# State outputs of an S5 layer: two channel groups in one f32 product of 128 partitions and 80 columns

## The chip, the core and the metric

The kernel runs on one core of a Trainium2 chip. The metric is the device time of one execution in microseconds (us). The engines of the core run side by side, each through its own list of instructions, and wait for one another only through semaphores: PE (TensorE, matrix products), DVE (VectorE), ACT (ScalarE), POOL (GpSimd) and SP (SyncE, which here only issues transfers). A product is two things on PE: a load of weights (the stationary operand, listed as PEld) and a stream of columns (the moving operand).

## The reference

One step of a hybrid encoder layer for 320 tokens (256 of a prompt, 64 of a running stream), model width 2048. After a norm, one projection gives q, k, v for eight heads of differential attention and the input u of an S5 state space model. Both results go through an output projection and a residual, and then through PEER, a mixture of 16,384 single-neuron experts. What the change touches is the S5 part:

```python
bu_r = jnp.einsum('blgp,gnp->blgn', uf, bbar_r)
bu_i = jnp.einsum('blgp,gnp->blgn', uf, bbar_i)
pr, pi, hr, hi = lax.associative_scan(combine, (a_r, a_i, bu_r, bu_i), axis=1)
...
y = (jnp.einsum('blgn,gpn->blgp', hr, c_re.astype(f32))
     - jnp.einsum('blgn,gpn->blgp', hi, c_im.astype(f32))
     + d_skip.astype(f32).reshape(SSM_GROUPS, SSM_P) * uf)
y = jax.nn.gelu(y.reshape(B, L, SSM_WIDTH))
```

There are 64 channel groups of 16 channels, and each drives a complex state of 64 numbers. The outputs also hold the final states.

## The kernel before

**The S5 part in chunks.** The 320 tokens are 40 chunks of 8 tokens. Within a chunk the outputs are a product of the chunk's own inputs with a matrix `Tm[:, g, :]` (8 tokens x 16 channels = 128 rows, 128 columns) for each group g. What comes from earlier chunks is a product of the state at the chunk's start with the output matrix times powers of the step. The state has 64 real and 64 imaginary numbers, and two groups share the 128 partitions: the even group has partitions 0 to 63, the odd one 64 to 127. `HCt` holds the states, first 32 group pairs of real parts, then 32 of imaginary parts, 40 chunks each. `CA[..][0]` and `CA[..][1]` are the real and imaginary output matrices of four group pairs at a time, in two buffers; DVE computes the first (`output_powers`), POOL the second.

So a group takes three f32 products into the same 40 columns of a PSUM bank: one over 128 rows (`Tm`) and two over its half of 64 rows (`CA` with `HCt`). That is `group_outputs` (L1600, L1601, L1602).

**The order.** The work of the front part is written out by hand along one index p. Step p is one quarter (512 columns) of a block of projection weights. Each weight is split into a high and a low part: ACT makes the high part of step p (`high_piece`, L497), DVE the low part (`front_low`, L864 on `w_parts`), and PE multiplies both with the tokens (`token_rows`, L1516 to L1522, eight products of 512 columns per step). `w_parts` has four buffers, so ACT can make the high part of step p once PE has done the token products of step p - 4. Everything else is hung on steps: each engine's loop over p asks which extra pieces belong to that step, and does them after its weight piece.

Around the change these are:
- steps 36 to 51: `own_kernels`, four f32 products of 32 columns with weights of 128x128 (L1546, L1547)
- steps 66 to 79: `kernels_moved` on PE (L1583) shifts one piece of `Tm` through PSUM, and `kernels_out` on ACT (L532) takes it out; piece i is moved in step 66 + i and taken out at ACT's turn 70 + i, and PE starts piece i only when piece i - 2 is out
- steps 74 to 76: `carry_inside` on DVE finishes the states of three of five segments (`HP`); step 77: `states_turned` (L1079) copies `HP` into `HCt`; steps 78, 79, 87, 91, ... 107: `output_powers`
- steps 80 to 111: two `group_outputs` a step on PE
- steps 81 to 89 and 101 to 109: the norms of the heads of q and of k, squares and roots on ACT, the rest on DVE
- steps 95, 96, 107, 108, 115: `y_out` on ACT, a gelu from PSUM into `Yb`; steps 109 and 116: `y_save`, eight transfers each, issued by ACT's queue. POOL fetches them back as `yT`.

Tiles live in one large array `experts` at fixed words, so a tile's place decides when it may be written.

Of the kernel before, what the change touches and what calls it, by code (L numbers as in the profile page):

```python
# [13 lines left out]
ACT = mybir.ActivationFunctionType  # L14
AX = mybir.AxisListType

P = 128
# [12 lines left out]
STEP = 8  # L30
# [55 lines left out]
def build(nc, io):  # L86
# [8 lines left out]
    with ctx:  # L95
# [152 lines left out]
        def bank(b, n=COLS):  # L248
            return psum[:, b, 0:n]
# [4 lines left out]
            u_out u_sv ug cbx in_out in_fold lam_e lam s5dt s5exp s5sin wx cbd k7mm k7o tm_mm tm tz  # L254
            wt_tr wt f_mm fs hp hc h_out ca cb y_mm y_gl y_sv0 y_sv1 y_in0 y_in1
            qsq hvar hstd q_ok k_ok qk_tr qkT v_out k_out cache zeros
# [75 lines left out]
        def _(sp):  # L332
# [91 lines left out]
        def _(pool):  # L424
# [16 lines left out]
            pool.wait_ge(S["k7o"], 3)  # L441
            pool.tensor_copy(Tm[:, :, P - SSM_P:], k7.rearrange("p (g n) -> p g n", g=GROUPS)).then_inc(S["tz"], 1)
# [4 lines left out]
            pool.wait_ge(S["hc"], 1)  # L447
            for x in range(8):
# [40 lines left out]
        def _(act):  # L489
# [18 lines left out]
            def project_out(c, n):  # L508

                (t0, r), m = TILES[n], NT * c + n  # L510
                if c < 4:
                    dst = (q_tok, k_tok)[c // 2][0:r, n, 512 * (c % 2):512 * (c % 2) + 512]
                else:
                    dst = v_tok[c - 4][0:r, n, :]
                act.wait_ge(S["w_used"], 4 * (8 + 4 * c + 4))
                if n < 2:
# [10 lines left out]
            def kernels_out(i):  # L527
                j, half = divmod(i, 2)
                n = SSM_P * (j + 1)
                act.wait_ge(S["tm_mm"], i + 1)  # L530
                act.wait_ge(S["tz"], 1)
                act.activation(Tm[0:n, 32 * half:32 * half + 32, 16 * j:16 * j + 16], psum[0:n, 6 + half, :].rearrange("p (g n) -> p g n", g=GP),  # L532
                               ACT.Copy).then_inc(S["tm"], 1)

            def squares(kind, n):

                r = TILES[n][1]
                m = NT * kind + n
                act.wait_ge(S["in_out"], NT * (2 * kind + 2))
                act.wait_ge(S["in_fold"], 2 * kind + 2)  # L540
                if m:
                    act.wait_ge(S["hvar"], m)
                else:
                    act.wait_ge(S["hc"], 1)
                act.activation(sq_head[0:r, :], (q_tok, k_tok)[kind][0:r, n, :], ACT.Square).then_inc(S["qsq"], 1)
# [6 lines left out]
            def y_out(f):  # L552

                trio, par = divmod(f, 2)
                k = min(12, GP - 12 * trio)
                act.wait_ge(S["y_mm"], min(3 * trio + 3, 8))
                if f == 0:
                    act.wait_ge(S["h_out"], 32)
                act.activation(Yb.rearrange("p (a b) c -> p b a c", b=2)[:, par, 12 * trio:12 * trio + k, :],
                               bank(4 + f % 4, CH * k).rearrange("p (g c) -> p g c", g=k),  # L560
                               ACT.Gelu_apprx_tanh).then_inc(S["y_gl"], 1)

            def y_save(half):
                act.wait_ge(S["y_gl"], 4 + 2 * half)
# [17 lines left out]
            def exponentials(u):  # L582
                n = u // HEADS
                act.wait_ge(S["s_mx"], u + 1)
                r, kk = TILES[n][1], KEYS_OF[n]
# [78 lines left out]
            for p in range(16, 4 * B_PQ + 1):  # L664
# [195 lines left out]
        def _(dve):  # L860
# [217 lines left out]
            def states_turned():  # L1078
                dve.tensor_copy(HCt.rearrange("p x (s c) -> p x s c", s=SEGS),  # L1079
                                HP[:, :, 0:SEG, :].rearrange("p s c x -> p x s c")).then_inc(S["hc"], 1)  # L1080

            def output_powers(x):

                rr, ri, cre, cim, ncim = ca_parts(x)
                dve.wait_ge(S["hc"], 1)
# [107 lines left out]
            for p in range(4 * B_PQ):  # L1193
# [294 lines left out]
        def _(pe):  # L1488
# [95 lines left out]

            def group_outputs(g):
                x, par, gp = g // 8, g % 2, g // 2
                fill = 2 * (gp // 12) + par
                if g == 0:
                    pe.wait_ge(S["tm"], 14)
                    pe.wait_ge(S["tz"], 2)  # L1590
                    pe.wait_ge(S["fs"], 6)
                    pe.wait_ge(S["hc"], 1)
                if g % 8 == 0:
                    pe.wait_ge(S["ca"], x + 1)
                    pe.wait_ge(S["cb"], 3 * x + 3)
                if gp % 12 == 0 and fill >= 4:
# [6 lines left out]
                if g % 8 == 7:  # L1603
                    ins.then_inc(S["y_mm"], 1)
# [119 lines left out]
            for p in range(4 * B_PQ):  # L1724
# [44 lines left out]
                if Y_AT <= p < Y_AT + 32:  # L1769
                    group_outputs(2 * (p - Y_AT))  # L1770
                    group_outputs(2 * (p - Y_AT) + 1)
                if QKT_AT <= p < QKT_AT + 6:
# [209 lines left out]
```

## Time and profile before

| | us |
|---|---|
| median of 3 runs | 2347.05 (2345.45 to 2352.65) |
| the profiled execution | 2347.72 |
| its span (first to last instruction) | 2345.9 |
| PE busy in the span | 2253.5 (96%) |
| DVE, ACT, POOL busy | 1678.6, 1091.8, 575.2 |

The profile comes from one execution. Its own time is 0.7 us above the median. Where a row has the form "start, length, engine, line, operation", the start is in us from the span's start. A product in f32 appears as two entries (x2). Products are pipelined: the length of one overlaps its successor, so that the cost of a product is read from one start to the next. A bracket at the end of a row tells how long the engine was idle before it and who ended the wait.

### The profile page before, as it was taken

The page shows a single profiled execution, that of the slowest core. Times are in us where ns is not written, and L with a number is a line of the kernel's source. Part 1 is how long each engine was busy: PE and PEld are TensorE (multiplying, and loading weights), DVE is VectorE, ACT ScalarE, POOL GpSimd, SP SyncE. Part 2 cuts the span into 40 slices and gives each one's busy share as a digit, 9 for nine tenths or more (in the row PEclk, how much of TensorE's full clock was granted, in tenths as well). Part 3 has the DMA queues.
Part 4 walks back from the last instruction along what each step waited for, and adds up shares of the span by engine and source line. Part 5 has one row for each costly group of instructions (what it writes and reads, how often), then busy time and mean ns, then how long its engine had stood idle before and what let it go on. Part 6 is the DMA issues. An engine that isn't in the chain of part 4 may idle for free.

```text
span 2345.9 us, 43355 instructions
## 1 busy us (share of the span) xinstructions
PE 2253.5 (96%) x17133; PEld 2158.4 (92%) x17133; DVE 1678.6 (72%) x2869; ACT 1091.8 (47%) x1999; POOL 575.2 (25%) x437
## 2 busy tenths in 40 slices
PE   7899999899899989999799999999999999999998
PEld 7785887779899989999799999999999999999998
DVE  7947864665455872886388888777678888777856
ACT  4234335654344544554344444444444444444444
POOL 3002320000176897559011111111001111111000
PEclk9999999999999999999899999999999999999999
DMA  6542235223343544776788988888778888888864
GB/s 226 120 113 73 90 94 197 96 90 126 144 161 127 171 156 159 242 219 219 237 320 329 360 335 306 311 307 335 270 274 335 342 326 323 313 323 318 311 213 153
DMA packets 128078, 537.69 MB, mean 229 GB/s; under 512 B 27648, under 2 KB 63920, under 8 KB 67216
## 3 DMA queue, kind: packets, MB, share of 16 engines
q1 hardware_dynamic: 61888, 358.62, 43.7%
q0 software_dynamic: 19200, 136.70, 14.0%
q10 hardware_dynamic: 46864, 40.71, 5.6%
q8 instruction: 77, 1.26, 0.2%
q14 instruction: 49, 0.40, 0.1%
HBM read 507.02 MB, written 28.38 MB: 228 GB/s over the span
## 4 chain that ended last, share of the span: by engine, by line
PE 61%; issue 19%; POOL 12%; DVE 5%; DMA 1%; ACT 1%; ACTq 0%; POOLq 0%; DVEq 0%
PE psum L1492 17%; PE psum L1494 17%; PE psum L1493 17%; POOL w_parts L473 12%; DVE experts L864 3%; PE psum L1516 2%; DVE w_parts L864 1%; PE psum L1518 1%; PE psum L1517 1%; DMA experts<-xs_tmp 1%; PE psum L1601 1%; PE psum L1600 1%; PE psum L1521 1%; PE psum L1602 1%; PE psum L1522 1%
## 5 line engine op out<-in xcount | busy, mean ns | idle before, releaser
L497 ACT ACTIVATE w_parts<-ring 128x512 fp32r<-128x512 f32 x1296 | 817.4, 632 | 1062.4 <-PE psum L1494 886.7
L864 DVE TENSOR_TENSOR w_parts<-ring,w_parts 128x512 fp32r<-128x512 f32 x1040 | 710.7, 695 | 477.5 <-ACT w_parts L497 467.3
L1492 PE MATMUL psum<-x_parts,w_parts 128*128 128x256 f32 (+1 forms) x2624 | 775.5, 296 | 30.2 <-POOL w_parts L473 13.6
L1494 PE MATMUL psum<-x_parts,w_parts 128*128 128x256 f32 (+1 forms) x2624 | 760.9, 290 | 0.0
L1493 PE MATMUL psum<-x_parts,w_parts 128*128 128x256 f32 (+1 forms) x2624 | 760.8, 290 | 0.0
L1492 PE MATMUL psum<-h_parts,w_parts 128*128 128x256 f32 x2048 | 582.0, 284 | 16.1 <-DVE h_parts L864 16.1
L1493 PE MATMUL psum<-h_parts,w_parts 128*128 128x256 f32 x2048 | 581.5, 284 | 0.0
L1494 PE MATMUL psum<-h_parts,w_parts 128*128 128x256 f32 x2048 | 581.4, 284 | 0.0
L1492 PEld LDWEIGHTS psum<-x_parts,w_parts 128*128 128x128 f32 x2624 | 504.5, 192 | 40.0 <-issue 17.4
L1493 PEld LDWEIGHTS psum<-x_parts,w_parts 128*128 128x128 f32 x2624 | 504.8, 192 | 0.7
L1494 PEld LDWEIGHTS psum<-x_parts,w_parts 128*128 128x128 f32 x2624 | 504.3, 192 | 0.0
L1492 PEld LDWEIGHTS psum<-h_parts,w_parts 128*128 128x128 f32 x2048 | 395.3, 193 | 16.7 <-issue 8.8
L473 POOL TENSOR_TENSOR w_parts<-ring,w_parts 128x512 fp32r<-128x512 f32 x256 | 358.5, 1414 | 208.7 <-ACT w_parts L497 203.2
L1493 PEld LDWEIGHTS psum<-h_parts,w_parts 128*128 128x128 f32 x2048 | 395.3, 193 | 0.0
L1494 PEld LDWEIGHTS psum<-h_parts,w_parts 128*128 128x128 f32 x2048 | 395.2, 193 | 0.0
L864 DVE TENSOR_TENSOR experts<-experts 128x256 f32<-128x256 f32 (+10 forms) x329 | 195.8, 605 | 8.2 <-ACT experts L626 2.9
L485 POOL DMA_INDIRECT experts<-in_peer_v,experts x64 | 73.8, 1153 | 480.1 <-DVE experts L1430 393.2
L485 POOL DMA_INDIRECT experts<-in_peer_u_rows,experts x64 | 73.3, 1145 | 460.6 <-DVE experts L1425 454.4
L1430 DVE SCALAR_TENSOR_TENSOR experts<-experts 128x2048 f32<-128x2048 f32 x63 | 147.7, 2345 | 0.0
L1425 DVE SCALAR_TENSOR_TENSOR experts<-experts 128x2048 f32<-128x2048 f32 x64 | 146.3, 2286 | 0.0
L864 DVE TENSOR_TENSOR experts<-psum,experts 128x1024 f32<-128x1024 f32 (+4 forms) x138 | 112.9, 854 | 13.6 <-PE psum L1494 12.4
L1516 PE MATMUL psum<-w_parts,x_parts 128*128 128x512 f32 x192 | 85.9, 447 | 9.6 <-DVE w_parts L864 9.1
(218 smaller groups left out, 1977.6 us busy)
## 6 DMA issues: line engine op xcount, KB each, us to landing
ring<-in_peer_u SPq DMA_DIRECT2D x128, 1024.0 KB, 4.8
ring<-in_peer_v SPq DMA_DIRECT2D x128, 1024.0 KB, 4.8
ring<-in_w_in SPq DMA_DIRECT2D x32, 1024.0 KB, 4.8
ring<-in_w_out SPq DMA_DIRECT2D x16, 1024.0 KB, 4.8
ring<-in_w_pq SPq DMA_DIRECT2D x16, 1024.0 KB, 4.9
g_tmp<-experts ACTq DMA_DIRECT2D x16, 1024.0 KB, 6.1
experts<-g_tmp ACTq DMA_DIRECT2D x16, 1024.0 KB, 6.7
experts<-in_xT SPq DMA_DIRECT2D x8, 640.0 KB, 9.0
```

The costliest lines, as they stand in the source:

```text
L473: pool.tensor_tensor(w_parts[:, q, 1, :], ring[:, k, 512 * q:512 * (q + 1)], w_parts[:, q, 0, :].bitcast(F32), ALU.subtract).then_inc(S["w ...
L485: pool.indirect_dma_start(rows[b], None, table, bass.IndirectOffsetOnAxis(ap=ids[:, k:k + 1], axis=0)).then_inc(S[f"gr{b}"], 16)
L497: act.activation(w_parts[:, q, 0, :], ring[:, b % SLOTS, 512 * q:512 * (q + 1)], ACT.Copy).then_inc(S["w_hi"], 1)
L864: return dve.tensor_tensor(out, a, b, op)
L1425: dve.scalar_tensor_tensor(row, row, 1.0, xs, ALU.mult, ALU.mult, accum_out=dots[:, k:k + 1]).then_inc(S["row_used"], 1)
L1430: dve.scalar_tensor_tensor(accs, row, coef[:, k:k + 1], accs, ALU.mult, ALU.add).then_inc(S["row_used"], 1)
L1492: pe.matmul(out, w_parts[:, q, 0, c], moving(0), start=start, stop=False)
L1493: pe.matmul(out, w_parts[:, q, 0, c], moving(1), start=False, stop=False)
L1494: return pe.matmul(out, w_parts[:, q, 1, c], moving(0), start=False, stop=stop)
L1516: pe.matmul(o, xh, w_parts[:, q, 0, :], start=dc == 0, stop=False)
L1517: pe.matmul(o, xh, w_parts[:, q, 1, :], start=False, stop=False)
L1518: pe.matmul(o, xl, w_parts[:, q, 0, :], start=False, stop=dc == DC - 1)
```

## The change

The states are laid out in two tiles `HB[0]` (real) and `HB[1]` (imaginary), with 80 columns for each group pair: the even group's 40 chunks in the first 40 columns on partitions 0 to 63, the odd group's in the last 40 on partitions 64 to 127, and zeros elsewhere. One product over 128 partitions then gives the sum for both groups, each in its own columns. `Tm` stays one product per group. Both copies are split by halves of the partitions: DVE copies the real parts, ACT the imaginary ones, and POOL writes the zeros. Since the tiles need room, `HP`, `Yb` and the order of the groups within `Tm` move, and some waits are added to guard the words that are used again.

```diff
-Q_NORM, Y_FILLS, O_NORM, O_TURN = (81, 101), (95, 96, 107, 108, 115, 115), (143, 157, 171), (167, 168, 169, 171, 174, 175)
+Q_NORM, Y_FILLS, O_NORM, O_TURN = (81, 101), (91, 95, 103, 107, 115, 115), (143, 157, 171), (167, 168, 169, 171, 174, 175)
...
-        HP = at(18432, SEGS * (SEG + 1), 2 * GP).rearrange("p (s c) x -> p s c x", s=SEGS)
+        HP = at(26320, SEGS * (SEG + 1), 2 * GP).rearrange("p (s c) x -> p s c x", s=SEGS)
-        HCt = at(0, 2 * GP, CH)
+        HB = [at(0, GP, 2 * CH), at(20480, GP, 2 * CH)]
-        Yb = at(20480, GROUPS, CH)
+        Yb = at(10752, GROUPS, CH)
...
+        def kernel_at(g):
+
+            return (g + GROUPS // 2) % GROUPS
+
+        def states_of(ri, par):
+
+            of = slice(64 * par, 64 * par + 64)
+            return (HB[ri][of, :, CH * par:CH * par + CH].rearrange("p x (s c) -> p x s c", s=SEGS),
+                    HP[of, :, 0:SEG, GP * ri:GP * ri + GP].rearrange("p s c x -> p x s c"))
...
             sp.dma_start(ckT, io["cache_k"]).then_inc(S["cache"], 16)
+            sp.wait_ge(S["y_sv0"], 16 * STEP)
+            sp.wait_ge(S["y_sv1"], 16 * STEP)
...
             pool.wait_ge(S["hp"], 1)
+            pool.wait_ge(S["tz"], 3)
+            for ri in range(2):
+                for par in range(2):
+                    if ri or par:
+                        pool.wait_ge(S["hz"], 2 * ri + par)
+                    pool.memset(HB[ri][64 * par:64 * par + 64, :, CH * (1 - par):CH * (1 - par) + CH], 0.0).then_inc(S["hz"], 1)
             pool.dma_start(io["states"][:, 0, :], HP[:, SEGS - 2, SEG, :]).then_inc(S["h_out"], 16)
...
+                if p == F_AT + 30:
+                    for par in range(2):
+                        act.wait_ge(S["hin"], 1)
+                        act.activation(*states_of(1, par), ACT.Copy).then_inc(S["hci"], 1)
                 if 0 <= p - TM_AT - 4 < 14:
                     kernels_out(p - TM_AT - 4)
...
             def states_turned():
-                dve.tensor_copy(HCt.rearrange("p x (s c) -> p x s c", s=SEGS),
-                                HP[:, :, 0:SEG, :].rearrange("p s c x -> p x s c")).then_inc(S["hc"], 1)
+                for par in range(2):
+                    dve.tensor_copy(*states_of(0, par)).then_inc(S["hc"], 1)
...
+                if p == F_AT + 28:
+                    dve.sem_inc(S["hin"], 1)
...
-                pr = slice(64 * par, 64 * par + 64)
-                out = psum[:, 4 + fill % 4, CH * (gp % 12):CH * (gp % 12) + CH]
-                pe.matmul(out, Tm[:, g, :], UG[:, g, :], start=True, stop=False)
-                pe.matmul(out, CA[x % 2][0][pr, gp % 4, :], HCt[pr, gp, :], start=False, stop=False)
-                ins = pe.matmul(out, CA[x % 2][1][pr, gp % 4, :], HCt[pr, GP + gp, :], start=False, stop=True)
+                out = psum[:, 4 + fill % 4, 2 * CH * (gp % 6):2 * CH * (gp % 6) + 2 * CH]
+                for par in range(2):
+                    pe.matmul(out[:, CH * par:CH * par + CH], Tm[:, kernel_at(2 * gp + par), :], UG[:, 2 * gp + par, :], start=par == 0, stop=False)
+                pe.matmul(out, CA[x % 2][0][:, gp % 4, :], HB[0][:, gp, :], start=False, stop=False)
+                ins = pe.matmul(out, CA[x % 2][1][:, gp % 4, :], HB[1][:, gp, :], start=False, stop=True)
```

(`F_AT` is 48 and `TM_AT` 66.) On PE, from the end of step 80's token products to the start of step 81's, before the change (L1600: `Tm`, L1601 and L1602: the states' real and imaginary products):

```order
L1522 MATMUL psum<-w_parts,x_parts 128x512
L1600 MATMUL psum<-experts 128x40 [waits hc,ca,fs,cb,tz,tm]
L1601 MATMUL psum<-experts 128x40
L1602 MATMUL psum<-experts 128x40
L1600 MATMUL psum<-experts 128x40
L1601 MATMUL psum<-experts 128x40
L1602 MATMUL psum<-experts 128x40
L1516 MATMUL psum<-w_parts,x_parts 128x512 [waits f_lo]
```

and with the change (L1631: `Tm`, L1632 and L1633: the states of both groups):

```order
L1551 MATMUL psum<-w_parts,x_parts 128x512
L1631 MATMUL psum<-experts 128x40 [waits hc,hci,hz,ca,fs,cb,tz,tm]
L1631 MATMUL psum<-experts 128x40
L1632 MATMUL psum<-experts 128x80
L1633 MATMUL psum<-experts 128x80
L1545 MATMUL psum<-w_parts,x_parts 128x512 [waits f_lo]
```

Six products became four, and the first also waits for the zeros (`hz`) and for ACT's copies (`hci`).

On ACT, turns 77 to 80, before (L497: high parts of the weights; L532: `Tm` pieces out of PSUM):

```order
L532 ACTIVATE experts<-psum 64x32x16 [waits tz,tm_mm]
L497 ACTIVATE w_parts<-ring 128x512 [waits w_used]
L532 ACTIVATE experts<-psum 80x32x16 [waits tz,tm_mm]
L497 ACTIVATE w_parts<-ring 128x512 [waits w_used]
L532 ACTIVATE experts<-psum 80x32x16 [waits tz,tm_mm]
L497 ACTIVATE w_parts<-ring 128x512 [waits w_used,slot0]
```

and with the change (L518 and L556 are the same two; L708 copies the imaginary states):

```order
L556 ACTIVATE experts<-psum 64x32x16 [waits tz,tm_mm]
L518 ACTIVATE w_parts<-ring 128x512 [waits w_used]
L708 ACTIVATE experts<-experts 64x32x40 [waits hin] x2
L556 ACTIVATE experts<-psum 80x32x16 [waits tz,tm_mm]
L518 ACTIVATE w_parts<-ring 128x512 [waits w_used]
L556 ACTIVATE experts<-psum 80x32x16 [waits tz,tm_mm]
```

The two copies stand between the high part of step 78 and piece 8 of `Tm`, and wait for DVE's `hin`.

## Rows read from the trace of the kernel before

**Rows 1.** The page: busy time by engine; the chain that ended last, by engine.

```profile
PE 2253.5 (96%) x17133; PEld 2158.4 (92%) x17133; DVE 1678.6 (72%) x2869; ACT 1091.8 (47%) x1999; POOL 575.2 (25%) x437
...
PE 61%; issue 19%; POOL 12%; DVE 5%; DMA 1%; ACT 1%; ACTq 0%; POOLq 0%; DVEq 0%
```

**Rows 2.** Busy time by stretch: PE, PEld, DVE, ACT, POOL, clock, DMA share, GB/s.

```profile
243.29:358.66 115.37, 115.37 (x633) 98.60 (x632) 80.12 (x116) 37.05 (x57) 27.19 (x19) 1.00 0.26 85
...
320.00:335.00 15.00, 15.00 (x84) 12.78 (x83) 14.43 (x24) 6.00 (x9) 3.63 (x3) 1.00 0.00 1
```

**Rows 3.** Order of time, PE, step 81: start us, us, engine, line, operation.

```profile
245.00 0.50 PE L1516 MATMUL psum<-w_parts,x_parts 128*128 128x512 f32 x1
...
246.95 0.31 PE L1600 MATMUL psum<-experts 128*128 128x40 f32 x2
...
247.75 0.42 PE L1600 MATMUL psum<-experts 128*128 128x40 f32 x2
...
248.10 0.41 PE L1601 MATMUL psum<-experts 64*128 64x40 f32 x2
...
248.66 0.50 PE L1516 MATMUL psum<-w_parts,x_parts 128*128 128x512 f32 x1
```

**Rows 4.** Order of time, PE, a step with four full-height f32 products.

```profile
118.25 0.30 PE L1546 MATMUL psum<-experts 128*128 128x32 f32 x2
...
119.06 0.48 PE L1516 MATMUL psum<-w_parts,x_parts 128*128 128x512 f32 x1
...
120.96 0.30 PE L1546 MATMUL psum<-experts 128*128 128x32 f32 x2
```

**Rows 5.** Order of time, PE, f32 products of other shapes.

```profile
40.81 4.47 PE L1529 MATMUL psum<-experts 128*128 128x320 f32 x16
...
160.38 0.67 PE L1571 MATMUL psum<-experts 128*64 128x40 f32 x16
```

**Rows 6.** Order of time, steps 76 to 79, and one stretch.

```profile
223.47 2.54 DVE L864 TENSOR_TENSOR experts<-experts 128x448 f32<-128x448 f32 x5
...
225.57 1.02 PE L1583 MATMUL psum<-experts,ident 128*96 128x512 f32 x2
...
230.31 1.05 ACT L545 ACTIVATE experts<-experts 128x1024 f32<-128x1024 f32 x1
...
236.00 0.79 PE L1516 MATMUL psum<-w_parts,x_parts 128*128 128x512 f32 x1 [3.23 <-DVE w_parts L864]
...
239.57 1.91 PE L1583 MATMUL psum<-experts,ident 128*112 128x512 f32 x2
...
236.00:241.00 5.00, 5.00 (x11) 3.36 (x11) 4.93 (x5) 1.19 (x2) 2.50 (x2) 0.50 0.60 210
```

**Rows 7.** Order of time, steps 88 to 110, and one stretch.

```profile
263.19 1.28 DVE L864 TENSOR_TENSOR w_parts<-ring,w_parts 128x512 fp32r<-128x512 f32 x2
...
301.14 0.73 DVE L864 TENSOR_TENSOR w_parts<-ring,w_parts 128x512 fp32r<-128x512 f32 x1 [4.98 <-ACT w_parts L497]
...
301.14:343.45 42.31, 42.31 (x234) 36.11 (x232) 37.01 (x54) 14.78 (x21) 11.69 (x9) 1.00 0.29 86
...
311.00 0.50 PE L1516 MATMUL psum<-w_parts,x_parts 128*128 128x512 f32 x1
...
338.18 5.56 ACTq L566 DMA_DIRECT2D y_tmp<-experts  x8
...
344.45 1.29 DVE L864 TENSOR_TENSOR w_parts<-ring,w_parts 128x512 fp32r<-128x512 f32 x2 [1.00 <-ACT w_parts L497]
```

**Rows 8.** Order of time: POOL's fill and first powers, the saved outputs, SP.

```profile
185.93 6.94 POOL L439 MEMSET experts<- 128x8192 f32 x1 [158.96 <-PE psum L1555]
...
229.21 1.49 POOL L452 TENSOR_TENSOR experts<-experts 128x512 f32<-128x512 f32 x1 [11.37 <-DVE experts L1079]
...
370.22 0.76 POOL L463 DMA_DIRECT2D experts<-y_tmp  x1 [22.99 <-DMA y_tmp<-experts]
...
390.94 0.42 SPq L366 DMA_DIRECT2D experts<-in_cache_k  x1
```

More of the change, by code:

```diff
@@ L254, in build @@
             u_out u_sv ug cbx in_out in_fold lam_e lam s5dt s5exp s5sin wx cbd k7mm k7o tm_mm tm tz
-            wt_tr wt f_mm fs hp hc h_out ca cb y_mm y_gl y_sv0 y_sv1 y_in0 y_in1
+            wt_tr wt f_mm fs hp hin hc hci hz h_out ca cb y_mm y_gl y_sv0 y_sv1 y_in0 y_in1
             qsq hvar hstd q_ok k_ok qk_tr qkT v_out k_out cache zeros
@@ L441, in _ @@
             pool.wait_ge(S["k7o"], 3)
-            pool.tensor_copy(Tm[:, :, P - SSM_P:], k7.rearrange("p (g n) -> p g n", g=GROUPS)).then_inc(S["tz"], 1)
+            for half in range(2):
+                pool.tensor_copy(Tm[:, kernel_at(32 * half):kernel_at(32 * half) + 32, P - SSM_P:],
+                                 k7[:, 512 * half:512 * half + 512].rearrange("p (g n) -> p g n", g=GP)).then_inc(S["tz"], 1)
             pool.wait_ge(S["hp"], 1)
+            pool.wait_ge(S["tz"], 3)
[4 more added lines that the diff above has]
+                    pool.memset(HB[ri][64 * par:64 * par + 64, :, CH * (1 - par):CH * (1 - par) + CH], 0.0).then_inc(S["hz"], 1)
             pool.dma_start(io["states"][:, 0, :], HP[:, SEGS - 2, SEG, :]).then_inc(S["h_out"], 16)
             pool.dma_start(io["states"][:, 1, :], HP[:, SEGS - 1, SEG, :]).then_inc(S["h_out"], 16)
-            pool.wait_ge(S["hc"], 1)
+            pool.wait_ge(S["hz"], 4)
+            pool.wait_ge(S["hc"], 2)
             for x in range(8):
@@ L515, in project_out @@
                 act.wait_ge(S["w_used"], 4 * (8 + 4 * c + 4))
+                if c == 2 and n == 0:
+                    act.wait_ge(S["hc"], 2)
+                    act.wait_ge(S["h_out"], 32)
                 if n < 2:
@@ L531, in kernels_out @@
                 act.wait_ge(S["tz"], 1)
-                act.activation(Tm[0:n, 32 * half:32 * half + 32, 16 * j:16 * j + 16], psum[0:n, 6 + half, :].rearrange("p (g n) -> p g n", g=GP),
+                act.activation(Tm[0:n, kernel_at(32 * half):kernel_at(32 * half) + 32, 16 * j:16 * j + 16], psum[0:n, 6 + half, :].rearrange("p (g n) -> p g n", g=GP),
                                ACT.Copy).then_inc(S["tm"], 1)
@@ L543, in squares @@
                 else:
-                    act.wait_ge(S["hc"], 1)
+                    act.wait_ge(S["hc"], 2)
                 act.activation(sq_head[0:r, :], (q_tok, k_tok)[kind][0:r, n, :], ACT.Square).then_inc(S["qsq"], 1)
@@ L552, in y_out @@
             def y_out(f):
[L554 to L560, printed above, removed]
+                k = min(6, GP - 6 * f)
+                act.wait_ge(S["y_mm"], -(-(6 * f + k) // 4))
+                act.activation(Yb[:, 12 * f:12 * f + 2 * k, :], bank(4 + f % 4, 2 * CH * k).rearrange("p (g c) -> p g c", g=2 * k),
                                ACT.Gelu_apprx_tanh).then_inc(S["y_gl"], 1)
             def y_save(half):
-                act.wait_ge(S["y_gl"], 4 + 2 * half)
+                act.wait_ge(S["y_gl"], 3 + 3 * half)
                 for j in range(STEP):
@@ L584, in exponentials @@
                 act.wait_ge(S["s_mx"], u + 1)
+                if u == 0:
+                    act.wait_ge(S["y_sv0"], 16 * STEP)
+                    act.wait_ge(S["y_sv1"], 16 * STEP)
                 r, kk = TILES[n][1], KEYS_OF[n]
@@ L1078, in states_turned @@
             def states_turned():
-                dve.tensor_copy(HCt.rearrange("p x (s c) -> p x s c", s=SEGS),
-                                HP[:, :, 0:SEG, :].rearrange("p s c x -> p x s c")).then_inc(S["hc"], 1)
+                for par in range(2):
+                    dve.tensor_copy(*states_of(0, par)).then_inc(S["hc"], 1)
             def output_powers(x):
                 rr, ri, cre, cim, ncim = ca_parts(x)
-                dve.wait_ge(S["hc"], 1)
+                dve.wait_ge(S["hc"], 2)
                 if x >= 2:
@@ L1583, in kernels_moved, with pair_outputs @@
                 pe.matmul(psum[0:n, 6 + half, :], ident[:, P - n:P], k7[:, 512 * half:512 * half + 512], start=True, stop=True).then_inc(S["tm_mm"], 1)
[L1585 to L1588, printed above, removed]
+            def pair_outputs(gp):
+                x, fill = gp // 4, gp // 6
+                if gp == 0:
                     pe.wait_ge(S["tm"], 14)
-                    pe.wait_ge(S["tz"], 2)
+                    pe.wait_ge(S["tz"], 3)
                     pe.wait_ge(S["fs"], 6)
-                    pe.wait_ge(S["hc"], 1)
-                if g % 8 == 0:
+                    pe.wait_ge(S["hz"], 4)
+                    pe.wait_ge(S["hc"], 2)
+                    pe.wait_ge(S["hci"], 2)
+                if gp % 4 == 0:
                     pe.wait_ge(S["ca"], x + 1)
                     pe.wait_ge(S["cb"], 3 * x + 3)
-                if gp % 12 == 0 and fill >= 4:
+                if gp % 6 == 0 and fill >= 4:
                     pe.wait_ge(S["y_gl"], fill - 3)
-                pr = slice(64 * par, 64 * par + 64)
-                out = psum[:, 4 + fill % 4, CH * (gp % 12):CH * (gp % 12) + CH]
-                pe.matmul(out, Tm[:, g, :], UG[:, g, :], start=True, stop=False)
-                pe.matmul(out, CA[x % 2][0][pr, gp % 4, :], HCt[pr, gp, :], start=False, stop=False)
-                ins = pe.matmul(out, CA[x % 2][1][pr, gp % 4, :], HCt[pr, GP + gp, :], start=False, stop=True)
-                if g % 8 == 7:
+                out = psum[:, 4 + fill % 4, 2 * CH * (gp % 6):2 * CH * (gp % 6) + 2 * CH]
[3 more added lines that the diff above has]
+                ins = pe.matmul(out, CA[x % 2][1][:, gp % 4, :], HB[1][:, gp, :], start=False, stop=True)
+                if gp % 4 == 3:
                     ins.then_inc(S["y_mm"], 1)
@@ L1769, in _ @@
                 if Y_AT <= p < Y_AT + 32:
-                    group_outputs(2 * (p - Y_AT))
-                    group_outputs(2 * (p - Y_AT) + 1)
+                    pair_outputs(p - Y_AT)
                 if QKT_AT <= p < QKT_AT + 6:
```

## The prediction

> **What bounds the kernel now.** I read the page's totals first: PE is busy for 96% of the span, and the chain of waits that ended last lies 61% on PE [rows 1]. So time taken off PE shortens the run wherever PE waits for nobody. Next the table by stretch: from 243.29 to 358.66 us, which are the 32 steps 80 to 111 with the state outputs, PE is busy for all of 115.37 us at the clock's upper level (1.00, 2.4 GHz), and DVE for 80.12 [rows 2]. PE bounds that stage alone. DVE's part isn't even, though: from 320 to 335 it is busy for 14.43 of 15 us [rows 2]. What PE gives back elsewhere can be lost to DVE there.
>
> Then one step in the order of time. Step 81 begins at 245.00 with its token products, begins its group products at 246.95 and ends at 248.66: 1.95 + 1.71 = 3.66 us [rows 3]. The 1.71 us hold six products (three for each group), each shown as two entries. One costs 0.24 to 0.35 us: the second full-height product starts at 247.75, and its successor of 64 rows at 248.10 [rows 3].
>
> **The change part by part. The products.** Six products a step become four: two of 40 columns as before, and two of 128 rows and 80 columns. No row of before has that form. The nearest is the stage at 118 us, where a step holds four f32 products with weights of 128x128 and 32 columns: they take 118.25 to 119.06 = 0.81 us, and the whole step 2.71 [rows 4]. Do 80 columns cost more than 32? Sixteen entries of 320 columns are busy for 4.47 us [rows 5], 0.28 us each or 0.87 ns a column, so that 80 columns stream for 0.07 us; an entry of the 0.81 us takes 0.10. The weights and not the columns set the pace, and 0.81 stands. The ends: below, sixteen entries with weights of 64 columns are busy for 0.67 us [rows 5], so eight take 0.34; above, four times the slowest full-height spacing, 4 x 0.35 = 1.40 us [rows 3]. I take 0.81, since its rows have the weights' shape and the count. A step then takes 1.95 + 0.81 = 2.76 us instead of 3.66, and 32 steps lose 32 x 0.90 = **28.8 us** (32 x 0.31 = 9.9 and 32 x 1.37 = 44 at the ends).
>
> That 64-row products beside each other could be worth more than full-height ones is what the Trainium skill says against this change: by "TensorE: Matmul & The Clock Gate", section "Part 3: Packing small matmuls — row/col tiling", a weight load slides under a running product only where the two use different row groups, and products in different row groups run together. The trace shows no such pairs before, since a full-height product stands between the two halves; the rows at 118 us have full-height loads one after the other at 0.10 us. If the rule held for the new form, the products would take the upper end above.
>
> **The wait at step 76.** ACT now copies the imaginary states in two pieces, at its turn 78, and waits there until DVE has finished the last segment. DVE's five operations from 223.47 take 2.54 us, so this ends at 226.01 [rows 6]. A copy of 1024 columns takes 1.05 us [rows 6], two of 1280 about 2.6, so ACT comes to the Tm piece at 228.7 and has it out at 229.3. PE's Tm product of step 76 started at 225.57 [rows 6] and needs this piece's bank: PE stands still for 3.7 us. Queued behind it on ACT are the Tm pieces and the high parts of the next steps. But PE already stood still 3.23 us before step 79 until 236.00, for DVE, and DVE is not later [rows 6]. The new idle eats the old one: after it the clock is at the lower level, 0.50 (1.2 GHz), as it was from 236 to 241 after the old idle [rows 6]; steps 77 and 78 run slowly instead of step 79, and PE comes to step 79 at about 237.6, done with it at 240.5 instead of 239.57. The last Tm piece is late by that, and the first pair starts at some 244.2 instead of 243.29: **+0.9 us**. Ends: 0, if DVE's 236.00 decides as before, and 3.7 + 2.5 = 6.2, if the idle and a fall of the clock come on top (a fall: the token part of step 79 took 236.00 to 239.57 = 3.57 instead of 1.95, the Tm product 1.91 instead of 1.02 [rows 6]).
>
> **DVE and ACT behind shorter steps.** Steps 81 to 89 (head norms of q): DVE had the low parts of steps 88 and 89 by 263.19 + 1.28 = 264.47, one after the other, so 88's by 263.85 [rows 7]. PE would come to step 88 at 244.2 + 0.81 + 7 x 2.76 = 264.3: just in time, nothing lost. Steps 99 to 109 (k): DVE began step 99's low part at 301.14, 9.86 us before PE began that step at 311.00 [rows 7]. From there to 343.45 it was busy 37.0 us [rows 7]; with about 1 us of gaps between instructions that is 38.0, its work for 11 steps, while PE will need 11 x 2.76 = 30.4. Its head start spans four buffers and shrinks by 4 x 0.90 to 6.3. So it comes to step 110's low part 38.0 - 6.3 = 31.7 after PE's step 99 and has it at 32.4; PE would want it at 30.4. ACT's eight DMA issues (5.56 us from 338.18) stand before its high part of step 110, which made DVE wait 1.00 us more, until 344.45 [rows 7]. Together **+3.0 us**, in two to four short stalls from step 104 to 110. The ends: 0, and 6 if POOL's products, which run beside DVE's, hit it harder than before.
>
> **At nothing.** DVE's turning copy keeps its element count (half the partitions, two pieces). POOL's four fills, some 1.1 us each by 6.94 us for 8192 columns, begin when the carried state is ready; there POOL was idle for 11.37 us up to 229.21 [rows 8], which hides their 4.4. Without that cover the first powers would be late by as much. The two Tm copies on POOL are the old one in halves. Two more table loads on ACT (the gelus moved to steps 91, 95, 103 and 107) cost it 2.6 us where DVE is later than ACT. On SP, the wait for the saved outputs stands before cache_v, the v outputs and the first w_out block: the save landed before 370.22, SP came there at 390.94 [rows 8], so 20 us cover it. The transfers from y back to yT follow PE's step 111 as before.
>
> **Sum.** -28.8 + 0.9 + 3.0 = -24.9 us, from the profiled execution's 2347.7 (span 2345.9) to 2322.8. The median of the runs is 2347.05, 0.7 less, so I say 2322. The following stages start from PE's step 112 and shift as a whole.
>
> **Rivals.** (1) DVE becomes the bound and the clock falls: stalls at 104 to 110 as long as the 3.23 us after which the clock was at 0.50 [rows 6] cost 2.5 each; two of them and 3 us more of DVE save 17 and give 2330. For it: DVE's 14.43 of 15 [rows 2]; against: the stalls come out near 1 us. (2) The full-height loads don't overlap: 9.9 - 0.9, no stall, 2338. Against it the rows at 118 us. (3) No stall at all: 2318; POOL and DVE would have to collide less. (4) The change doesn't do what it says, as where 80 columns cost what three products did: 2347, for which no row speaks. (5) Slower: short steps starve PE so often that the clock stays at 0.50 within the stage. A step then takes 3.57 + 2 x 0.81 = 5.2 us, 1.5 above today's; from 12 of the 32 steps on the gain is gone, and with 20 it is -0.9 x 12 + 1.5 x 20 = +19, 2366. Against it: a PE at half speed lets DVE catch up, so that the idle ends by itself.
>
> **Numbers.** Forecast 0.64 (its own range 2316 to 2328), rival 1 0.15, rival 2 0.08, rival 3 0.05, rival 4 0.04, rival 5 0.04. From 2315 to 2332 lie the forecast, rival 3 and most of rival 1: 0.82. A difference under 0.3% (7 us) can't be told from none: faster 0.92, the same 0.04, slower 0.04.
>
> **What would show it.** A step of the stage at 2.7 to 2.8 us with eight f32 entries in about 0.81; the idle of 3 to 4 us before the Tm product of step 76 and none left before step 79; the first pair near 244; PE waits for DVE of about a microsecond between steps 104 and 110; step 112 at about 334 instead of 358.66. An entry of 80 columns well above 0.10 us makes the forecast wrong, as does a stage in which DVE ends most of PE's waits.

## The result and the profile after

The changed kernel takes 2336.17 us (median of 6 runs, 2328.09 to 2337.88), the kernel before in the same rounds 2347.14 us. The ratio is 0.9942 (95%: 0.9929 to 0.9954), which is 13.6 us; the two medians are 11.0 us apart. The forecast was 2322, a gain of 24.9 us, with a range up to 2332. So about half of the gain came, and the time lies outside the range.

The profiled execution has 2328.09 us, the fastest of the six, so it shows less of what is missing than the median has; the run named again below gives a second profile. The page, busy time and the chain (compare [rows 1]):

```profile
PE 2223.3 (96%) x17005; PEld 2133.7 (92%) x17005; DVE 1676.9 (72%) x2870; ACT 1098.3 (47%) x2003; POOL 583.7 (25%) x442
...
PE 58%; issue 19%; POOL 12%; DVE 7%; DMA 1%; ACT 1%; ACTq 1%; POOLq 0%; DVEq 0%
```

PE lost 30.2 us of busy time, but the span only 19.7 (2345.9 to 2326.2); DVE's share of the chain rose from 5% to 7%. First the part that came out as forecast, one step of the stage in order of time (start, length, engine, line; L1631 Tm, L1632 and L1633 the two new products; compare [rows 3]):

```profile
247.52 0.53 PE L1631 MATMUL psum<-experts 128*128 128x40 f32 x4
247.89 0.43 PE L1632 MATMUL psum<-experts 128*128 128x80 f32 x2
248.15 0.39 PE L1633 MATMUL psum<-experts 128*128 128x80 f32 x2
248.33 0.47 PE L1545 MATMUL psum<-w_parts,x_parts 128*128 128x512 f32 x1
...
250.25 0.53 PE L1631 MATMUL psum<-experts 128*128 128x40 f32 x4
```

The f32 products take 247.52 to 248.33 = 0.81 us, a step 2.73. So the loss isn't in the products. Busy time by stretch (columns as in [rows 2]; the first row is the stage and compares with the first of [rows 2], the last row with its second):

```profile
244.67:339.34 94.67, 88.57 (x505) 76.83 (x506) 77.95 (x116) 38.35 (x58) 29.50 (x19) 0.98 0.31 100
...
255.00:265.00 10.00, 9.97 (x60) 8.62 (x59) 9.64 (x15) 1.42 (x4) 4.64 (x3) 1.00 0.26 80
265.00:275.00 10.00, 7.28 (x36) 6.16 (x37) 9.72 (x15) 4.11 (x7) 6.06 (x3) 0.90 0.09 31
...
270.00:275.00 5.00, 2.74 (x14) 2.26 (x13) 4.79 (x11) 0.63 (x1) 1.25 (x1) 0.81 0.05 8
...
275.00:285.00 10.00, 10.00 (x55) 8.56 (x54) 7.43 (x9) 2.46 (x4) 4.24 (x3) 0.92 0.53 194
285.00:320.00 35.00, 35.00 (x207) 30.66 (x206) 27.97 (x35) 19.87 (x28) 12.91 (x10) 1.00 0.19 64
320.00:335.00 15.00, 11.65 (x66) 9.83 (x65) 12.94 (x28) 3.05 (x6) 0.07 (x1) 1.00 0.51 115
```

PE has two holes. From 265 to 275 it is busy for 7.28 of 10 us and the clock's mean falls to 0.90, where DVE is full (9.72); from 320 to 335 it is busy for 11.65 of 15. In between DVE has slack. The beginnings of these holes, PE in order of time:

```profile
265.46 0.50 PE L1545 MATMUL psum<-w_parts,x_parts 128*128 128x512 f32 x1 [0.49 <-DVE w_parts L891]
...
273.42 0.79 PE L1545 MATMUL psum<-w_parts,x_parts 128*128 128x512 f32 x1 [2.26 <-DVE w_parts L891]
...
322.65 0.50 PE L1545 MATMUL psum<-w_parts,x_parts 128*128 128x512 f32 x1 [1.03 <-DVE w_parts L891]
...
326.62 0.50 PE L1545 MATMUL psum<-w_parts,x_parts 128*128 128x512 f32 x1 [1.01 <-DVE w_parts L891]
...
333.64 0.50 PE L1545 MATMUL psum<-w_parts,x_parts 128*128 128x512 f32 x1 [1.31 <-DVE w_parts L891]
```

These are steps 88, 90, 107, 108 and 110. The last three are the short stalls forecast for steps 104 to 110. The first two were not forecast. What DVE and POOL do ahead of them (DVE's rows, then POOL's):

```profile
253.98 6.08 DVE L891 TENSOR_TENSOR experts<-experts,small 128x1024 f32<-128x1024 f32 x6
...
261.35 2.01 DVE L891 TENSOR_TENSOR experts<-experts 128x512 f32<-128x512 f32 x3
...
266.20 5.80 DVE L891 TENSOR_TENSOR experts<-experts,small 64x1024 f32<-64x1024 f32 x6
...
272.67 1.29 DVE L891 TENSOR_TENSOR w_parts<-ring,w_parts 128x512 fp32r<-128x512 f32 x2
...
254.16 2.03 POOL L473 TENSOR_TENSOR experts<-experts 128x512 f32<-128x512 f32 x1 [16.31 <-PE psum L1633]
...
265.12 1.87 POOL L473 TENSOR_TENSOR experts<-experts 128x512 f32<-128x512 f32 x1 [5.39 <-PE psum L1633]
```

The same pieces in the kernel before, which the prediction had not read together:

```profile
252.43 3.42 DVE L864 TENSOR_TENSOR experts<-experts,small 128x1024 f32<-128x1024 f32 x6
...
257.83 4.00 DVE L864 TENSOR_TENSOR experts<-experts 128x512 f32<-128x512 f32 x3
...
327.10 6.30 DVE L864 TENSOR_TENSOR experts<-experts,small 128x1024 f32<-128x1024 f32 x6
...
256.21 1.14 POOL L452 TENSOR_TENSOR experts<-experts 128x512 f32<-128x512 f32 x1 [17.63 <-PE psum L1602]
...
329.55 1.11 POOL L452 TENSOR_TENSOR experts<-experts 128x512 f32<-128x512 f32 x1 [9.83 <-PE psum L1602]
```

Before, the second q norm was over at 252.43 + 3.42 = 255.85 and POOL began its set at 256.21. POOL is released by PE, and the faster PE released it at 254.16; DVE, which began the stage later, came to the norm at 253.98. Now they run side by side and the norm takes 6.08 us. The third q norm meets the next set too (5.80). After it come the low parts of steps 90 and 91 (from 272.67), for which PE has waited 2.26 us.

The meeting itself isn't new, and its price stood in the trace before: there POOL's set at 256.21 ran beside DVE's own `output_powers` (4.00 us; 2.01 in the changed kernel), and its last set, from 329.55, beside the second k norm (6.30 us). PE filled the stage, so neither cost time. In the changed kernel the k norms take 3.41, 4.23 and 3.39 us, and DVE's busy time in the stage is even lower (77.95 us against 80.12). What changed is where the stretch falls. The second q norm's 2.66 us more are made up at once by the shorter powers and low part behind it: from its start to the low parts of steps 88 and 89 DVE needs 10.75 us (253.98 to 264.73), as before (252.43 to 263.19). The third norm's 2.4 us aren't made up before step 90's low part.

The beginning of the stage, ACT and PE (compare [rows 6]):

```profile
225.07 4.83 ACT L708 ACTIVATE experts<-experts 64x1280 f32<-64x1280 f32 x2 [6.10 <-DVEq L1286]
229.92 0.59 ACT L556 ACTIVATE experts<-psum 80x512 f32<-80x512 f32 x1
...
230.66 1.99 PE L1612 MATMUL psum<-experts,ident 128*96 128x512 f32 x2 [5.95 <-ACT experts L556]
...
244.67 0.64 PE L1631 MATMUL psum<-experts 128*128 128x40 f32 x4 [0.63 <-ACT experts L556]
```

ACT's two copies take 4.83 us, not 2.6, so PE stands still for 5.95 us before step 76's Tm product, not 3.7; no idle is left before step 79. The first pair starts at 244.67 (forecast 244.2, before 243.29). Behind the stage this profile shows no change: from its end to the end of the span it takes 2326.2 - 339.34 = 1986.9 us here and 2345.9 - 358.73 = 1987.2 before. POOL's four fills (4.82 us at 215.42, after 21.9 us of idle) and its first powers (228.39) are no later than in [rows 8].

### The profile page after: what moved, and what is told of

Same layout as the page of the kernel before. It is cut to its first block, busy times and chain, and to the rows that moved or that the text cites. A ratio compares the mean times of both kernels' runs of the same rounds, so it can differ in the third digit from the quotient of the medians.

```text
span 2326.2 us, 43114 instructions
## 1 busy us (share of the span) xinstructions
PE 2223.3 (96%) x17005; PEld 2133.7 (92%) x17005; DVE 1676.9 (72%) x2870; ACT 1098.3 (47%) x2003; POOL 583.7 (25%) x442
## 4 chain that ended last, share of the span: by engine, by line
PE 58%; issue 19%; POOL 12%; DVE 7%; DMA 1%; ACT 1%; ACTq 1%; POOLq 0%; DVEq 0%
PE psum L1521 17%; PE psum L1523 17%; PE psum L1522 17%; POOL w_parts L494 12%; DVE experts L891 4%; DVE w_parts L891 1%; PE psum L1545 1%; DMA experts<-xs_tmp 1%; PE psum L1547 1%; PE psum L1546 1%; DVE x_parts L906 1%; ACTq L586 0%; PE psum L1550 0%; PE psum L1551 0%; PE psum L1528 0%
## 5 line engine op out<-in xcount | busy, mean ns | idle before, releaser
L518 ACT ACTIVATE w_parts<-ring 128x512 fp32r<-128x512 f32 x1296 | 816.9, 632 | 1023.6 <-PE psum L1523 883.1
L1521 PE MATMUL psum<-x_parts,w_parts 128*128 128x256 f32 (+1 forms) x2624 | 775.2, 295 | 30.5 <-POOL w_parts L494 13.6
```

The costliest lines, as they stand in the source:

```text
L518: act.activation(w_parts[:, q, 0, :], ring[:, b % SLOTS, 512 * q:512 * (q + 1)], ACT.Copy).then_inc(S["w_hi"], 1)
L1521: pe.matmul(out, w_parts[:, q, 0, c], moving(0), start=start, stop=False)
```

## The experiments

Each run was timed in five rounds beside the kernel before. "Stage" is the time in the profile from the first pair of state outputs to the last. Two theories of the missing gain stand against each other: A, ACT's copies and PE's wait for them take it; B, DVE, slowed by POOL's products beside it, makes PE wait within the stage.

| run | median us | ratio (95%) | first pair | stage us | clock in it |
|---|---|---|---|---|---|
| before, profiled | 2347.05 | | 243.29 | 115.44 | 1.00 |
| changed, profiled | 2336.17 | 0.9942 (0.9929 to 0.9954) | 244.67 | 94.67 | 0.98 |
| again | 2334.28 | 0.9933 (0.9919 to 0.9946) | 245.15 | 96.67 | 0.96 |
| copy_later | 2328.93 | 0.9913 (0.9900 to 0.9926) | 242.18 | 96.60 | 0.96 |
| pool_small | 2322.54 | 0.9896 (0.9881 to 0.9910) | 244.63 | 86.05 | 1.00 |
| q_later | 2339.27 | 0.9958 (0.9946 to 0.9971) | 244.77 | 99.86 | 0.95 |
| before_pool_small | 2346.98 | 0.9998 (0.9989 to 1.0007) | 244.97 | 115.55 | 1.00 |
| six_products | 2337.15 | 0.9956 (0.9943 to 0.9970) | 243.77 | 100.17 | 1.00 |
| k_later | 2334.23 | 0.9948 (0.9934 to 0.9962) | 246.60 | 90.83 | 0.98 |
| copy_k_later | 2330.72 | 0.9934 (0.9920 to 0.9947) | 243.21 | 90.83 | 0.98 |
| q_spread | 2328.85 | 0.9908 (0.9895 to 0.9922) | 245.06 | 90.61 | 1.00 |
| copy_q_spread | 2322.98 | 0.9898 (0.9880 to 0.9916) | 241.98 | 90.49 | 1.00 |
| copy_qk_spread | 2322.75 | 0.9886 (0.9871 to 0.9901) | 241.99 | 87.36 | 1.00 |

**again**: the changed kernel, unedited.

> The changed kernel once more, for a second profile and more times. Theory A (ACT's wait for the states at its turn 78 and its slower copies take the missing gain, 5.95 us of PE idle before the Tm product of step 76): every execution has this idle, so the times lie within 3 us of each other near 2328. Theory B (DVE, slowed by POOL's products beside it, makes PE wait in the steps with the head norms, and PE's clock falls to its lower level after some of these waits): the idle at step 76 is the same in both profiles, and the times spread over 2328 to 2338, with a lower mean clock where they are longer.

Measured: 2334.28 us. The waits stand where they stood (265.94, 273.89, 323.28, 327.25 and 334.53), the last with a further fall of the clock behind it. The twelve executions of both runs spread from 2326.16 to 2337.88 us, the fastest with the highest mean clock (0.988) and the slowest with the lowest (0.981): wider than theory A has it, and in the way of theory B.

**copy_later**: ACT's copies go three turns later, behind that turn's Tm piece; the first output of the k projection, which is written over `HP`, waits for them.

```diff
-                if p == F_AT + 30:
+                if 0 <= p - TM_AT - 4 < 14:
+                    kernels_out(p - TM_AT - 4)
+                if p == F_AT + 33:
                     for par in range(2):
...
-                if 0 <= p - TM_AT - 4 < 14:
-                    kernels_out(p - TM_AT - 4)
```

> The changed kernel with ACT's two copies moved from turn 78 to turn 81, behind that turn's Tm piece. Theory A: no idle before step 76's Tm product, the first pair at 243.4 instead of 244.7, and most of the missing gain comes back: 2322 to 2326. Theory B: PE then waits some 3.2 us before step 79 for DVE as in the kernel before, the first pair comes about 1 us earlier, and the time falls by 0 to 2 us only.

Measured: 2328.93 us, 5.4 less than the changed kernel beside it. The first pair starts at 242.18, 3.0 earlier than there; the stage itself (96.60) and its waits stay. The gain lies between the two theories' numbers (8 to 12 us for A, 0 to 2 for B). So ACT's wait costs, but it isn't what is missing in the stage.

**pool_small**: POOL's sets from the third on are cut to 1/32 of their columns, so that a part of the outputs is left out.

```diff
+                few = slice(0, 4 if x < 2 else 1), slice(0, STEP if x < 2 else 1)
+                cut = lambda ap: ap[:, few[0], few[1], :]
-                pool.tensor_tensor(ca_cols(CA[x % 2][1]), rr, ncim, ALU.mult).then_inc(S["cb"], 1)
+                pool.tensor_tensor(cut(ca_cols(CA[x % 2][1])), cut(rr), cut(ncim), ALU.mult).then_inc(S["cb"], 1)
...
```

> The changed kernel with POOL's output powers cut to a thirty-second of their size from the third set on (a part of the outputs is then left uncomputed). Theory B: DVE's head norms take 3.4 us each instead of 6.1 and 5.8, the waits of PE before steps 88 to 90 and 108 to 111 (0.5 + 2.3 + 3 x 1.1 us, and 1.4 for the lower clock) fall to under 2 us in all, and the time is 5 to 9 us lower, 2320 to 2330. Theory A: DVE's waits don't decide, and the time stays within 2 us.

Measured: 2322.54 us, which is near the forecast's 2322 by another sum (no wait in the stage, and outputs left out). The stage by stretch, and the third q norm in order of time (5.80 us in the changed kernel):

```profile
244.63:330.68 86.05, 86.05 (x505) 75.41 (x506) 63.93 (x116) 38.92 (x58) 11.07 (x19) 1.00 0.35 112
```

```profile
263.52 3.43 DVE L893 TENSOR_TENSOR experts<-experts,small 64x1024 f32<-64x1024 f32 x6
```

PE is busy for the whole stage, and all five waits are gone, though DVE has the same instructions: its busy time is 63.93 us instead of 77.95. This is the plainest case for theory B.

**before_pool_small**: the same cut in the kernel before.

> A control: the kernel before (not the changed one), with POOL's output powers from the third set on cut to 1/32 of their columns, so that part of the outputs is not computed. In the changed kernel the same cut gained 12 us. Theory B (POOL's products cost something only where DVE has no slack left): before the change PE fills the whole stage, so the cut gains nothing: 2346 to 2349. Rival: POOL's products cost time anywhere, by a port or memory that PE or the transfers need too, or by delaying the state outputs themselves: several us gained here too, 2336 to 2342.

Measured: 2346.98 us, ratio 0.9998. DVE's busy time in the stage falls from 80.12 to 65.87 us here too, and it is worth nothing where PE fills the stage. So what POOL's products take there, they take from DVE.

**q_later**: the q norms start seven steps later, with two gelus moved out of their way.

```diff
-Q_NORM, Y_FILLS, O_NORM, O_TURN = (81, 101), (91, 95, 103, 107, 115, 115), (143, 157, 171), (167, 168, 169, 171, 174, 175)
+Q_NORM, Y_FILLS, O_NORM, O_TURN = (88, 101), (97, 98, 103, 107, 115, 115), (143, 157, 171), (167, 168, 169, 171, 174, 175)
```

> The changed kernel with the norms of q moved from steps 81 to 89 to steps 88 to 96, where DVE has more free time, and the first two gelus from steps 91 and 95 to 97 and 98. Theory B: the waits before steps 88 and 90 (0.5 and 2.3 us) and the lower clock behind them (1.4 us) go, some of it comes back at 95 to 99, and the time falls by 2 to 5 us. Theory A: no difference over 1 us.

Measured: 2339.27 us, some 5 above the changed kernel: theory B's number missed. The waits moved with the norms (2.22 us before 283.71, 2.34 before 296.06), and from 280 to 310 the clock's mean was 0.83. Moving the bunch doesn't undo it.

**six_products**: each 80-column product is split into two of 40.

```diff
-                pe.matmul(out, CA[x % 2][0][:, gp % 4, :], HB[0][:, gp, :], start=False, stop=False)
-                ins = pe.matmul(out, CA[x % 2][1][:, gp % 4, :], HB[1][:, gp, :], start=False, stop=True)
+                for ri in range(2):
+                    for par in range(2):
+                        cols = slice(CH * par, CH * par + CH)
+                        ins = pe.matmul(out[:, cols], CA[x % 2][ri][:, gp % 4, :], HB[ri][:, gp, cols], start=False, stop=ri == 1 and par == 1)
```

> The changed kernel, with each full-height product of 80 columns split into two of 40 columns, with the same weights loaded twice: per step four products on the states instead of two, with the same columns in all. If the loads set the pace (0.10 us an entry, as the prediction took it): four entries more a step, 1.22 us instead of 0.81 for the f32 products, 3.15 us a step instead of 2.74. 32 x 0.41 = 13.1 us more on PE, of which the stalls for DVE (some 6.7 us with what the low clock costs) are hidden now: 2341 to 2348. If the columns set the pace: no change, 2334 to 2336.

Measured: 2337.15 us, between the two ranges. It is the rows of a step that decide. Two successive steps and the stage by stretch:

```profile
247.05 0.53 PE L1631 MATMUL psum<-experts 128*128 128x40 f32 x4
247.42 1.06 PE L1635 MATMUL psum<-experts 128*128 128x40 f32 x8
248.31 0.48 PE L1545 MATMUL psum<-w_parts,x_parts 128*128 128x512 f32 x1
...
250.24 0.53 PE L1631 MATMUL psum<-experts 128*128 128x40 f32 x4
```

```profile
243.77:343.94 100.17, 100.17 (x633) 89.67 (x634) 78.94 (x116) 39.45 (x58) 27.04 (x19) 1.00 0.30 98
```

The price per entry holds: twelve entries from 247.05 to 248.31 = 1.26 us, a step 3.19 instead of 2.73, with the same 480 columns. The run also splits the gain, which the prediction had only as a whole: the twelve entries before, eight of them with weights of 64 rows, took 1.71 us [rows 3], so half of the 0.90 us a step comes from the full height and half from four products in place of six. Why the entries of 64 rows were dearer, no run settles. But 32 x 0.46 = 14.7 us more for PE lengthened the stage by only 3.5 to 5.5 (from 96.67 or 94.67), since PE now never waits and the clock stays at 1.00. The expectation had put the stalls at 6.7 us; they cost about 10.

**k_later**: the norms of k start five steps later (`Q_NORM` (81, 106) instead of (81, 101)).

> The changed kernel, with the head norms of k moved from steps 101 to 109 to steps 106 to 114 (ACT's squares and roots and DVE's part). POOL's last set of powers then runs beside no norm of k, and the third norm lies behind step 111, the last with state outputs. Theory B (DVE is the bound of the stage: its work, stretched where POOL computes beside it, fills the time of the short steps): the waits of PE for DVE near 322, 327 and 334 us (1.0, 1.0, 1.3 us, and the low clock behind them) go; the waits at 265 and 273 stay. Some 4 us less than the changed kernel: 2329 to 2331. Theory A (ACT's wait and copies take the missing gain): no change, 2334 to 2336. A third outcome: the heads' turning at steps 114 to 119 waits for the later norms and gives the gain back.

Measured: 2334.23 us, no gain. The stage is shorter by 4 to 6 us (90.83) and the waits after 320 are gone, but the third outcome came. PE in the turning of the heads, in order of time:

```profile
345.49 1.03 PE L1647 MATMUL psum<-ident,experts 128*128 128x128 f32 x8
351.37 0.88 PE L1647 MATMUL psum<-ident,experts 128*128 128x128 f32 x3 [3.02 <-ACT experts L599]
```

The turning takes 342.8 to 363.0 instead of 344.7 to 359.6.

**copy_k_later**: both edits, copy_later's and k_later's.

> Both: ACT's copies of the imaginary states behind the Tm piece of turn 81, as in the run before that moved them, and the norms of k at steps 106 to 114. Theory B: the gains add up, about 5 us for the copies and 4 for the norms: 2324 to 2327, above the run with POOL's sets cut (2322.5) by what the waits at 265 and 273 cost, less than the copies gain. Theory A: as the run with the later copies alone, 2329.

Measured: 2330.72 us, no better than the later copies alone (2328.93). Theory B's number (2324 to 2327) missed, and between the theories this pair says nothing: a wait of 3.31 us in the turning of the heads came here too.

**q_spread**: the q norms come five steps apart, so that DVE's slack from 280 to 300 is used.

```diff
-                    n, late = divmod(p - Q_NORM[kind], 3)
+                    n, late = divmod(p - Q_NORM[kind], (5, 3)[kind])
```

> The changed kernel, with the head norms of q five steps apart instead of three (steps 81, 86 and 91 instead of 81, 84 and 87; the norms of k stay). DVE has time to spare between 280 and 300 us, and the norms go there. Theory B (DVE late because norms, its own powers and POOL's come in the same steps): PE's waits at 265 and 273 us (0.5 and 2.3 us) and the low clock behind them go, some 5 us less than the changed kernel: 2328 to 2331; the waits after 320 stay. Theory A (ACT's wait and copies take the missing gain): no change, 2334 to 2336. A third outcome: the norms meet POOL's sets and the later powers instead, as where they were moved by seven steps, and PE waits at 280 to 300.

Measured: 2328.85 us, as theory B had it: the waits near 265 and 273 are gone and the stage takes 90.61 us. DVE's busy time in it is what it was (78.44 against 77.95), and the third norm still meets a set of POOL's and takes 6.21 us, but PE doesn't wait for the low parts behind it. So what lacked was not DVE's time in sum but where it fell.

**copy_q_spread**: with the copies of copy_later.

> ACT's copies behind the Tm piece of turn 81, and the norms of q five steps apart. Theory B: both gains, 5 + 5 us less than the changed kernel, 2323 to 2327. Theory A: 2329, as with the copies alone.

Measured: 2322.98 us. The gains add up.

**copy_qk_spread**: and the k norms four steps apart, `(5, 4)[kind]`.

> As the run before it, and the norms of k four steps apart instead of three (steps 101, 105, 109). Theory B: the waits after 320 us shrink as well (1.0, 1.0 and 1.3 us now), 2 to 4 us less than with the norms of q alone: 2320 to 2325. If DVE's work in sum is what lacks there, and not its order: no change against the run before it, or the turning of the heads at step 119 waits for the last norm.

Measured: 2322.75 us, the best whole kernel of the study: 28.3 us below the kernel before beside it (2351.01), 24.3 below the 2347.05 shown ahead of the prediction, ratio 0.9886 (0.9871 to 0.9901). The stage by stretch:

```profile
241.99:329.35 87.36, 86.39 (x506) 75.45 (x505) 79.03 (x117) 40.23 (x60) 26.29 (x19) 1.00 0.35 109
```

Two waits of 0.26 and 0.72 us are left. The stage is 3.1 us shorter than with the q norms alone; the median doesn't show it, and in the profiled executions 3.8 us more behind the stage (1991.8 against 1988.0) outweigh it; what such differences are made of is told below.

## Why the prediction was wrong

**The products: right.** -28.8 us rested on [rows 3] and [rows 4]; the new ones take the forecast 0.81 us, and six_products shows on this kernel that it is the entry of full height that costs, 0.10 to 0.11 us, not the columns. The caution from the Trainium skill, "TensorE: Matmul & The Clock Gate", section "Part 3: Packing small matmuls — row/col tiling", that full-height weights would not slide under a running product, would have put the step near 3.4 us by the prediction's upper end (1.95 + 1.40, an estimate from [rows 3]); the trace has 2.73.

**The wait at step 76: right in kind, wrong in size.** Two copies of 64x1280 were priced by ACT's 1.05 us for 1024 columns [rows 6] and took 4.83 us instead of 2.6. The stage began 0.5 us later than forecast (1.0 in the second profile), +1.4 to +1.9 instead of +0.9. copy_later and copy_q_spread gained 5.4 and 5.9 us by moving the copies out of the way, of which 3 show at the first pair; the rest isn't in the stage and is not settled, since executions of one kernel differ as much behind it.

**The failed step: "Steps 81 to 89 (head norms of q) ... just in time, nothing lost", and with it the +3.0 us.** That term kept DVE's durations of before and ended its sum at step 89. The stalls for the k norms came as it said, and for its reasons (1.03 + 1.01 + 1.31 = 3.35 us, the last behind ACT's DMA issues). But POOL's sets are released by PE, so the faster PE moved them into the q norms: the third norm took 5.80 us instead of the 3.43 of pool_small, 2.4 more, and stands before step 90's low part; PE waited 2.26 us. DVE also came to these norms 1.5 us later than before, as the stage began later, which makes the 0.49 us before step 88. Behind the wait of 2.26 us the clock's mean was 0.81 from 270 to 275, and the token products of the step took 273.42 to 276.78 = 3.36 us instead of 1.92. In all the stage lost 94.67 - 86.05 = 8.6 us in one execution and 96.67 - 86.05 = 10.6 in the other, instead of 3.0. q_spread, without the two waits for the q norms, has 90.61: so about 4.1 of the 8.6 belong to the q norms, put at nothing, and about 4.6 to the k norms, put at 3.0. The second profile's further 2.0 are the fall of the clock behind the wait before step 110. pool_small, the control before_pool_small and q_spread show this cause by three different edits. The loss is the upper end of this term (6, if POOL's products hit harder) with rival 1's fall of the clock on top; rival 1 had the kind of loss right, and its place (steps 104 to 110) in the second profile only.

By the Trainium skill, "SBUF — State Buffer", section "SBUF: two separate sides", VectorE and GpSimd lock a pair of ports against each other for a whole instruction, where VectorE reads two operands from SBUF and GpSimd reads there too. The rows agree in kind: norms of 3.4 us alone and 5.8 to 6.1 beside POOL, whose first operation of a set takes 1.87 to 2.03 us there and 1.11 to 1.37 in the later four sets.

**What stays open.** The profiled execution missed the forecast by 5.3 us, and all of that lies in the stage and its start; that it came out within the range is luck, since the median missed by 14. The second profile (2335.89 us) is close to the median. It is 0.5 us later at the stage's start, 2.0 longer in the stage, and behind it has 1992.3 us against 1986.9, where the prediction let the following stages "shift as a whole". The same stretches of work, in the first profile and then in the second:

```profile
385.00:400.00 15.00, 13.03 (x75) 11.87 (x76) 6.80 (x21) 5.66 (x21) 0.00 (x0) 0.89 0.76 288
1130.00:1140.00 10.00, 10.00 (x72) 10.00 (x73) 4.90 (x9) 3.47 (x6) 0.00 (x0) 0.84 0.34 111
2285.00:2295.00 10.00, 7.84 (x66) 7.64 (x65) 7.11 (x13) 3.88 (x7) 0.00 (x0) 1.00 0.34 120
```

```profile
387.50:402.50 15.00, 13.11 (x67) 11.95 (x68) 6.10 (x21) 5.24 (x19) 0.00 (x0) 0.77 0.76 288
1135.00:1145.00 10.00, 9.90 (x60) 9.90 (x61) 4.55 (x9) 2.83 (x5) 0.00 (x0) 0.69 0.30 105
2291.50:2301.50 10.00, 7.84 (x53) 7.65 (x53) 6.32 (x12) 2.95 (x5) 0.00 (x0) 0.83 0.32 115
```

In each stretch PE gets fewer products done in the second profile, at a lower clock. The three cost 1.2, 1.1 and 1.4 us of the 5.4, and two waits for DVE ahead of the second one (9.01 and 6.00 us instead of 8.56 and 5.43) another 1.0. The work itself did shift as a whole; the clock and these waits didn't. That isn't of the change: before_pool_small, with 1989.1 us behind the stage against 1987.2 before, has such a late fall of the clock too. Why the clock falls in one execution and not in another, and why the changed kernel's median lies among the longer ones, no run settles.

## What to carry to other kernels

When the bounding engine gets faster, read every instruction that it releases on the other engines at its new time and see what it now runs beside; a duration taken from the trace before holds only for its old neighbours, and the price of the new ones may stand elsewhere in that trace, as the k norm's 6.30 us did here. A mean share of busy time (DVE's 78 of 95 us) says nothing on a helper that works in bunches: sum its work up to each deadline, past the last piece of the bunch. And a gain that got lost in such a bunch comes back by spreading the pieces, not by moving all of them.

## What was not expected of the hardware

The same wait was followed by a lower clock in one execution and not in another. In copy_later and in copy_qk_spread PE stands still for 3.26 us before step 79 (until 235.54 and 235.37); the next 10 us in the two:

```profile
235.00:245.00 10.00, 9.17 (x36) 6.35 (x36) 9.86 (x13) 7.71 (x12) 3.06 (x2) 0.83 0.37 120
```

```profile
235.00:245.00 10.00, 7.91 (x38) 6.06 (x38) 9.86 (x13) 6.78 (x12) 2.89 (x2) 1.00 0.37 120
```

The two ran on different chips, but copy_q_spread, on the chip of copy_qk_spread and with the same instructions up to there, stands still until 235.37 as well and has 0.83 from 235 to 245. At 0.83 and at 1.00 the first pair comes at the same time, 242.18 and 241.99: PE at the full clock then waits 1.72 us for DVE, at the lower one 0.28. And ACT is slower than DVE at one and the same shape: two copies of 64x1280 into rows of 80 columns, 4.83 us on ACT and 2.51 on DVE, which does its two in the row below.

```profile
225.73 2.51 DVE L1107 COPY experts<-experts 64x1280 f32<-64x1280 f32 x2
```
